# Two experts' main rows computed during the last routing, in a hybrid decoder step with a mixture of experts

## What is computed

```python
def moe(h, w_router, b_router, w_gate, w_up, w_down):
    aff = sigmoid(h @ w_router)                       # 16 experts in 4 groups
    biased = aff + b_router
    gscore = top_k(biased.reshape(n, 4, 4), 2)[0].sum(-1)
    in_group = ... == argmax(gscore, -1)[:, None]     # one group a token
    _, idx = top_k(where(in_group, biased, NEG_INF), 2)
    w_sel = take_along_axis(aff, idx, -1); w_sel /= w_sel.sum(-1)
    ...
    hid = silu(a) * b * gates                         # a = h @ w_gate[e], b = h @ w_up[e]
    return einsum('nef,efd->nd', hid, w_down)

h = layer_norm(ALPHA * x + mix @ w_out)               # mix: attention, state space, pooling
y = layer_norm(ALPHA * h + moe(h))
```

## Time and profile before

| | |
|---|---|
| median of 3 runs | 997.49 us (997.23 to 998.46) |
| the profiled execution | 994.33 us, span 992.6 us |
| TensorE (PE) | busy 912.7 us, 92% of the span |
| VectorE (DVE) | busy 423.7 us, 43% |
| ScalarE (ACT) | busy 311.8 us, 31% |
| GpSimd (POOL) | busy 212.7 us, 21% |
| mean granted PE clock | 0.978 of full |
| DMA | 173.23 MB, 175 GB/s in the mean |

### The profile page before, as it was taken

How to read it: one execution, slowest core, us unless ns; L and a number is a source line. 1 busy time by engine, 2 the same in 40 slices (tenths; PEclk the granted TensorE clock), 3 DMA queues, 4 the chain that set the end, 5 groups by cost and what they waited for, 6 DMA issues and landing times.

```text
span 992.6 us, 13623 instructions
## 1 busy us (share of the span) xinstructions
PE 912.7 (92%) x5025; PEld 579.4 (58%) x5025; DVE 423.7 (43%) x1244; ACT 311.8 (31%) x631; POOL 212.7 (21%) x289
## 2 busy tenths in 40 slices
PE   4999999999999999999899999994899999999785
PEld 4655645555566666666554444532788887878321
DVE  5689799612344343345424326648100001010156
ACT  6751505612233233225414233431212121211222
POOL 3089000011101346651021100432000000000155
PEclk9999999999999999999999999996999999999888
DMA  9540000465982025216441131457976888966293
GB/s 232 156 182 1 2 0 2 143 188 168 413 352 88 22 77 181 107 64 226 159 171 45 43 87 45 169 207 279 318 244 242 319 301 288 380 220 254 95 373 138
DMA packets 63677, 173.23 MB, mean 175 GB/s; under 512 B 17416, under 2 KB 26687, under 8 KB 58103
## 3 DMA queue, kind: packets, MB, share of 16 engines
q1 hardware_dynamic: 55047, 141.37, 41.0%
q0 software_dynamic: 8368, 30.41, 8.4%
q10 hardware_dynamic: 192, 0.52, 0.2%
HBM read 113.24 MB, written 59.11 MB: 174 GB/s over the span
## 4 chain that ended last, share of the span: by engine, by line
PE 43%; DVE 3%; ACT 2%; DMA 1%; issue 1%; ACTq 0%; POOL 0%; DVEq 0%
PE banks L2350 14%; PE banks L2185 11%; PE banks L2363 6%; PE banks L2465 2%; PE banks L2344 2%; PE banks L2376 1%; PE banks L2482 1%; PE banks L2296 1%; PE banks L2197 1%; PE banks L2269 1%; PE banks L2250 1%; PE banks L2217 1%; DVE xT L2744 0%; DMA x_slots<-xT,slot_i 0%; DVE arena L2814 0%
## 5 line engine op out<-in xcount | busy, mean ns | idle before, releaser
L1514 PE MATMUL banks<-xT,arena 128*128 128x384 f32 (+2 forms) x384 | 122.9, 475 | 5.7 <-DVE mx L1709 3.8
L2185 PE MATMUL banks<-arena,mixT 128*128 128x512 f32 x256 | 116.8, 602 | 0.0
L1514 PEld LDWEIGHTS banks<-xT,arena 128*128 128x128 f32 x384 | 71.4, 190 | 53.6 <-DVE mx L1709 10.5
L2185 PEld LDWEIGHTS banks<-arena,mixT 128*128 128x128 f32 x256 | 47.0, 193 | 49.5 <-issue 49.5
L2350 PEld LDWEIGHTS banks<-mixT,arena 128*128 128x128 f32 x512 | 70.4, 190 | 6.8 <-issue 6.8
L2350 PEld LDWEIGHTS banks<-mixT,v_tok 128*128 128x128 f32 x512 | 70.3, 190 | 4.3 <-issue 4.3
L2350 PE MATMUL banks<-mixT,arena 128*128 128x160 f32 x512 | 71.7, 300 | 0.8 <-ACT mixT L2564 0.8
L2350 PE MATMUL banks<-mixT,v_tok 128*128 128x160 f32 x512 | 70.9, 299 | 0.8 <-ACT mixT L2564 0.8
L2721 POOL DMA_INDIRECT arena<-y_park,slot_s x17 | 16.2, 951 | 250.6 <-DMA y_park<-arena 245.7
L1619 ACT ACTIVATE arena<-arena,mx 128x144 f32<-128x144 f32 (+7 forms) x64 | 50.2, 785 | 62.5 <-DVE mx L1709 62.1
L535 PE MATMUL banks<-mixT,xT 128*128 128x512 f32 x144 | 62.7, 594 | 0.0
(11 more groups left out here) (413 smaller groups left out, 1367.5 us busy)
## 6 DMA issues: line engine op xcount, KB each, us to landing
arena<-in_w_down SPq DMA_DIRECT2D x16, 1024.0 KB, 8.4
x_slots<-xT SPq DMA_DIRECT2D x4, 2048.0 KB, 15.4
y_park<-xT SPq DMA_DIRECT2D x4, 2048.0 KB, 32.5
v_tok<-in_w_gate SPq DMA_DIRECT2D x8, 1024.0 KB, 7.0
v_tok<-in_w_up SPq DMA_DIRECT2D x8, 1024.0 KB, 7.0
arena<-in_w_gate SPq DMA_DIRECT2D x8, 1024.0 KB, 6.4
arena<-in_w_up SPq DMA_DIRECT2D x8, 1024.0 KB, 8.6
arena<-x_slots SPq DMA_DIRECT2D x16, 512.0 KB, 5.3
```

What stands on the lines that cost most here:

```text
L1514: last = T.matmul(b[:, 0:cn], w[:, k, :], xT[:, k, c0:c0 + cn], start=(k == 0), stop=(k == KD - 1))
L2185: last = T.matmul(bank[half], mixT[:, k, META + t * P:META + (t + 1) * P], w_oh[half][:, k, :], start=(k == 0), stop=(k == KD - 1))
```

## The change

- Batches become (0, 4), (4, 6), (6, 7), (7, 9). `choose(2)` and `slots(2)`, now for tile 6 alone, come into DVE's turn of tile 7; PE's `ranks(1)` and `ranks(2)` come into tile 7, and tile 6's two scatters follow directly on those of tiles 4 and 5 on POOL. The last batch has tiles 7 and 8.
- For experts 0 and 1 (`FIRST = 2`) the 128 main places are for tiles 0 to 6; before batch 3 their counts are raised to 128, so tiles 7 and 8 (and what is beyond 128) go to the 32 last places.
- The samples' projection writes banks 6 and 7, not 0 and 1, and no longer waits for tile 7's residual.
- SP loads the main rows of experts 0 and 1 as soon as tiles 0 to 6 are scattered, behind three of the weight loads; PE turns the rows of expert 0 ahead of tile 8, runs its gate matmuls between the steps of tile 8's routing, then its up matmuls, `ranks(3)`, expert 1 and both down passes, all on 128 rows. The eight idle matmuls are gone.
- The 32 last rows of experts 0 and 1 are then computed together, with the weights moving and the rows standing (`first_rests`): four groups (gate and up of both) side by side. The product is transposed back (`turn_first_rests`) and put beside the other hidden rows.
- Buffers for this: expert 2's gate and up weights have their own places; the gate and up weights of experts 3 and 4 wait for `first_rests`; main rows of experts 0 to 3 have buffers of their own. All four loads of rest rows of the first group are issued on SP (two were on ACT). The second norm's gain and shift are loaded later.
- At the end ACT makes `scaled_i` and the 18 `dg` before expert 15's silu; PE runs `residual` of tiles 1, 3 and 0 before the overflow block, as their banks come free, and of tile 2 after it. The square root table is loaded ahead. Tile 8's second norm is done in two DVE passes, without ACT's.
- At the start `centre(1)` comes before `dt_rows`, and `copy_high(0)` before `stats(2)`.

```diff
-NOV = 2 * TOKM // (CAP + 1)
+FIRST = 2
+NOV = FIRST + (2 * TOKM - FIRST * (REM + 1)) // (CAP + 1)
...
                 stats(1)
+                centre(1)
                 dt_rows()
-                centre(1)
+                copy_high(0)
                 stats(2)
-                copy_high(0)
...
-            BATCH = ((0, 4), (4, 6), (6, 8), (8, 9))
+            BATCH = ((0, 4), (4, 6), (6, 7), (7, 9))
+            EARLY = BATCH[2][1]
...
                 def load_gate(e):
-                    if e >= 2:
+                    if e == 2:
+                        sp.wait_ge(s_mm, NT)
+                    elif 3 <= e <= 4:
+                        sp.wait_ge(s_fr, 1)
+                    elif e >= 5:
                         sp.wait_ge(s_gt, e - 1)
...
                 def load_rows(e):
-                    if e >= 2:
+                    if e < FIRST:
+                        sp.wait_ge(s_sct, 16 * 2 * EARLY)
+                        sp.wait_ge(s_mm, NQ)
+                    elif e < 4:
+                        sp.wait_ge(s_sct, 16 * 2 * NT)
...
                 load_gate(0)
                 load_up(0)
                 load_gate(1)
+                load_rows(0)
+                load_rows(1)
                 load_up(1)
                 load_down(0)
                 load_down(1)
+                load_gate(2)
+                load_up(2)
+                load_down(2)
+                load_rest(0)
+                load_rows(2)
+                load_down(3)
+                load_rows(3)
+                store(0)
+                store(1)
+                load_gate(3)
+                load_up(3)
+                load_rest(1)
+                load_gate(4)
+                load_up(4)
...
+                def first_rests():
+                    pe.wait_ge(s_hid, FIRST)
+                    for k in range(KD):
+                        for which in range(2):
+                            for e in range(FIRST):
+                                g = 2 * which + e
+                                last = T.matmul(bank[2][REM * g:REM * (g + 1), 0:DE], xall[:, e, k, MAIN:CAP],
+                                                (gate_w, up_w)[which](e)[:, k * DE:(k + 1) * DE],
+                                                start=(k == 0), stop=(k == KD - 1), tile_position=(0, REM * g))
+                    last.then_inc(s_fr, 1)
...
+                t = NT - 2
+                turn(t - 1)
+                project(t, 0)
+                route_parts(t - 1)
+                turn_probabilities(3)
+                ranks(1)
+                project(t, 1, slice(0, 2))
+                route(t - 1)
+                project(t, 1, slice(2, 4))
+                weigh(3)
+                project(t, 2)
+                turn_outputs(3)
+                ranks(2)
+                project(t, 3)
+                t = NT - 1
+                project(t, 0)
+                project(t, 1)
+                turn(t - 1)
+                project(t, 2)
+                route_parts(t - 1)
+                project(t, 3)
+                route(t - 1)
+                pe.wait_ge(s_xe[0], 16)
+                turn_rows(0, xe[0])
+                turn(t)
+                pe.wait_ge(s_gw[0], 16)
+                pe.wait_ge(s_xc, 2)
+                pe.wait_ge(s_res, NT)
+                gate_or_up(0, 0, js=(0,))
+                route_parts(t)
+                gate_or_up(0, 0, js=(1,), ks=range(0, 4))
+                route(t)
+                gate_or_up(0, 0, js=(1,), ks=range(4, KD)).then_inc(s_gt, 1)
+                pe.wait_ge(s_xe[1], 16)
+                turn_rows(1, xe[1])
+                pe.wait_ge(s_uw[0], 16)
+                gate_or_up(0, 1).then_inc(s_up, 1)
                 ranks(3)
-                for n in range(8):
-                    T.matmul(bank[n % 2], ident[:, :], mixT[:, 0, META:META + 512], start=True, stop=True)
...
+                gate_or_up(1, 0).then_inc(s_gt, 1)
+                pe.wait_ge(s_uw[1], 16)
+                gate_or_up(1, 1).then_inc(s_up, 1)
+                down(0)
+                down(1)
                 pe.wait_ge(s_xr, 64)
...
+                turn_rows(rest_no(0), xr)
+                pe.wait_ge(s_xe[2], 16)
+                turn_rows(turn_no(2), xe[2])
+                pe.wait_ge(s_xc, 2 * rest_no(0) + 2)
+                first_rests()
...
                 pe.wait_ge(s_al, 1)
-                for t in range(4):
-                    residual(t)
+                residual(1)
+                pe.wait_ge(s_yA, out_no(E - 1))
+                pe.wait_ge(s_yD, out_no(E - 1))
+                residual(3)
...
+                residual(0)
...
+                overflow(pe, released, body, done)
+
+                residual(2)
...
+                S.activation(ln[2][:, 18:19], ident[:, 0:1], ACT.Sqrt).then_inc(s_tl, 1)
+                act.wait_ge(s_mm, NT)
+                copy_rows(0)
+                x_turned(NT - 1)
+                deviation(NT - 1)
+                S.activation(ln[2][:, 19:20], ident[:, 0:1], ACT.Exp).then_inc(s_tl, 1)
+                take_parts(NT - 1)
+                take_logits(NT - 1)
+                copy_rows(1)
+                silu(0)
+                silu(1)
+                low(0, ys[0])
+                low(1, ys[1])
...
+                    if t0 == EARLY:
+
+                        chain(V.scalar_tensor_tensor(prior[:, t0, 0:FIRST], cap16[:, 0:FIRST], float(MAIN),
+                                                     prior[:, t0, 0:FIRST], ALU.add, ALU.max))
...
-                    if t == 8:
-                        choose(2, residual_samples)
+                    if t == 7:
+                        choose(2)
                     if dec and t % 2:
                         outputs(d)
+                    if t == 7:
+                        slots(2)
...
+                hidden(0)
                 weights(2)
                 weights(3)
                 overflow_table()
+                hidden(1)
...
+                high(0, ys[0])
+                high(1, ys[1])
```

More of the change, by code:

```diff
@@ L1891, in hybrid_step @@
             hid = [mall[:, at + 2 * CAP * n:at + 2 * CAP * (n + 1)].rearrange("p (j n) -> p j n", j=2) for n in range(6)]
+            at += 12 * CAP
+            sil = [mall[:, at + 2 * CAP * n:at + 2 * CAP * (n + 1)] for n in range(2)]
+            at += 4 * CAP
+            hr = mall[HP:P, at:at + DE]
+            assert 7 * TP <= at - 4 * CAP and at - 7 * TP <= META + SEQ and at + DE <= KD * TP
+            xe = [mixT[:, 3, 0:D], mixT[:, 4, 0:D], gb[:, 0, :], gb[:, 1, :]]
+            assert 3 * TP >= 2 * KD * CAP
             gate_src = A["w_gate"][0].rearrange("e (p k) f -> e p (k f)", p=P)
@@ L2183, in project @@
                     else:
-                        for k in range(4 * (quarter % 2), 4 * (quarter % 2) + 4):
+                        for k in range(4 * (quarter % 2), 4 * (quarter % 2) + 4)[part_]:
                             last = T.matmul(bank[half], mixT[:, k, META + t * P:META + (t + 1) * P],
@@ L2379, in down_rest @@
                     last.then_inc(s_dn, 1)
-                for t in range(NT):
-                    d, dec = t // 2, t < BS
-                    if dec and t % 2 == 0:
+                for t in range(NT - 2):
+                    d = t // 2
+                    if t % 2 == 0:
                         turn_keys(d, 0)
@@ L2444, in _, with residual @@
                 down_rest(E // 4 - 1)
+                def residual(t):
+                    if t - 4 in SHIFT_DVE:
+                        pe.wait_ge(s_yv, shifted_no(t - 4))
+                    elif t >= 4:
+                        pe.wait_ge(s_gn2, t - 3)
+                    for half in range(2):
+                        cols = slice(512 * half, 512 * half + 512)
+                        T.matmul(duo[t % 4][:, cols], scaled_i, h_all[:, t, cols],
+                                 start=True, stop=False)
+                pe.wait_ge(s_al, 1)
+                residual(1)
+                pe.wait_ge(s_yA, out_no(E - 1))
+                pe.wait_ge(s_yD, out_no(E - 1))
+                residual(3)
+                pe.wait_ge(s_yA, out_no(E - 1) + 1)
+                pe.wait_ge(s_yD, out_no(E - 1) + 1)
+                residual(0)
                 pe.wait_ge(s_yA, out_no(E - 1) + 2)
@@ L2973, in _ @@
                 measure(NT - 1)
-                slots(2)
                 scale_shift(NT - 1)
```

309 lines of the change are left out of this document (184 added, 125 removed).

## The result

The changed kernel takes **1303.05 us** (median of 4 runs, 1299.4 to 1308.31) beside 997.36 (996.5 to 998.46) for the kernel before: 1.308 times as long, interval 1.304 to 1.312. The forecast was 969.4 us, 963.5 to 976.5. The profiled execution took 1308.31 us, with a span of 1306.6.

A forecast was written before the change was run, and what follows sets the result against it. PE (TensorE) was taken as busy nearly everywhere, its largest hole where the last tokens are routed. Gains 1.4 + 20.7 + 6.0 = 28.1 us off 997.5 gave 969.4 us, range 963.5 to 976.5.

The forecast's parts named there:

- the parts don't fit: Experts 0 and 1 drawing over 128 early or 32 late rows would run the overflow pass; called excluded, no chance given.
- slower than before: Last tokens' routing: expert 0's rows landing past 700.6 would lose the gain; at 703 the time is 1000; chance 0.02.
- Start: First tiles: tile 1 given first lets PE turn it 1.5 to 2.0 us earlier; gain kept 1.4 (0 to 2.0).
- The cover named there: Early in the kernel DVE meets a load at 37.75 that the change doesn't move, so not all of 1.5 to 2.0 is kept.
- Middle: Last tokens' routing up to expert 3's gate: work of experts 0 and 1 fills PE's hole; gain 20.7 us.
- rows come late: Tile 6's scatter needs the whole 9.0 us, expert 0's rows at 675.1; 2.6 us less gain, 972.0; chance 0.25.
- the forecast's own sign of being wrong: In routing, PE waiting over 3 us for expert 0's rows, tile 6's ranks or expert 3's weights.
- Clock: Near 670, where PE has only transposes, its clock falls; this decides 2.3 us of the routing gain.
- New stalls: Late weights of experts 3 and 4 cost 2.1; with a low tail and no start gain, 974.8; chance 0.11.
- Tail: After the experts: residuals in PE's standing time, tile 0 3.5 us sooner, shorter last tile; gain 6.0 (4.1 to 7.6).
- the old hole: Kernel before, samples' output projection to expert 0's first gate matmul: 33.5 us, with PE busy for 16.9.
- alone: Scatters with no weight loads beside them, taken to land in 3.8 us, against 9.0 beside six weight loads.

The follow-up runs named there:

- the version with real rows: Changed kernel with the last batch's ranks and counts taking 64 rows for tile 8, so its padding rows aren't counted; 970.33 us, 971.88 when run again.
- the run with earlier rows: Against the version with real rows: expert 1's gate weights loaded behind experts 0 and 1's first rows, expert 2's rows issued from ACT's queue; 973.03 us.

## Why the prediction was wrong, and where it was right

**The step that failed** is the last rival, *the parts don't fit*: "excluded". In its place the overflow pass ran for two experts and cost 332.7 us (1303.05 against 970.33 with real rows counted). The working there was a count of the reference's own choices for experts 0 and 1. It asked whether real tokens fit their places and took for granted that the kernel counts only these. It didn't follow the new batch into `ranks`, where the number of rows goes by a batch's first tile, and it looked at the two experts that the change handles, not at 13 and 14, which stand at 159 and 157 of 160 and needed two and four more. So a chance of nothing stood on a branch whose price, 166 us an expert, the trace of before couldn't show. The 0.02 for slower than before stood for late rows.

**The rest of the sum** can be checked on the version with real rows. Stretches of the kernel before that answer to it, from the last quarter of tile 7's projection: to expert 3's gate, to the last rest rows, to tile 0's weights, to the end.

```profile
656.00:740.48 84.48, 65.69 (x366) 47.01 (x365) 34.18 (x136) 19.09 (x38) 10.92 (x10) 0.90 0.83 298
740.48:929.32 188.84, 187.31 (x1162) 150.84 (x1160) 18.11 (x30) 33.17 (x78) 0.00 (x0) 1.00 0.75 270
929.32:949.10 19.78, 13.34 (x50) 4.88 (x49) 1.38 (x2) 5.78 (x21) 8.00 (x9) 0.83 0.59 193
949.10:992.60 43.50, 29.08 (x89) 8.80 (x88) 31.04 (x66) 13.69 (x19) 22.24 (x15) 0.84 0.63 246
```

The same stretches with real rows:

```profile
656.90:723.14 66.24, 57.22 (x416) 41.92 (x416) 30.79 (x115) 20.06 (x40) 8.00 (x7) 0.97 0.87 311
723.14:912.11 188.97, 187.25 (x1161) 150.84 (x1161) 17.42 (x29) 36.90 (x96) 0.00 (x0) 1.00 0.78 287
912.11:928.77 16.66, 10.94 (x49) 3.83 (x49) 1.38 (x2) 2.66 (x4) 5.73 (x6) 0.95 0.52 163
928.77:970.10 41.33, 28.88 (x88) 8.83 (x88) 30.66 (x65) 11.24 (x17) 24.46 (x17) 0.83 0.73 285
```

- *Start, 1.4 (0 to 2.0)*: nothing. PE's first long projection starts at 15.46 in place of 17.14, as forecast, but DVE then meets tile 6's input, the load of the earlier trace rows, at 39.29 and not 37.75 (37.9 to 42.3 in the nine other profiles of the new order), and at 50 us PE is level with before (50.11 and 49.91). The last quarter of tile 7's projection begins 0.9 later (0.2 in the second profile of this version). The cover named there took all of it.
- *Middle, 20.7 (17 to 23)*: 84.48 - 66.24 = 18.2; 18.9 in the second profile of this version (65.57). The steps, on the timeline of the version with real rows:

```profile
660.88 0.96 POOL L2857 DMA_INDIRECT x_slots<-xT,slot_i  x1 [0.30 <-issue]
671.14 0.80 SPq L2130 DMA_DIRECT2D mixT<-x_slots  x2
674.81 1.97 PE L2421 MATMUL banks<-ident,mixT 128*128 128x128 f32 x8 [4.99 <-DMA mixT<-x_slots]
692.10 0.98 POOL L2857 DMA_INDIRECT x_slots<-xT,slot_i  x1 [19.26 <-DVE slot_i L3074]
699.82 1.92 SPq L2140 DMA_DIRECT2D arena<-x_slots  x4
704.77 1.16 PE L2421 MATMUL banks<-ident,arena 128*128 128x128 f32 x8
707.39 1.16 PE L2421 MATMUL banks<-ident,gb 128*128 128x128 f32 x8 [1.46 <-DMA gb<-x_slots]
712.07 4.61 PE L2430 MATMUL banks<-mixT,arena 128*128 128x160 f32 x32
723.14 8.93 PE L2430 MATMUL banks<-mixT,arena 128*128 128x160 f32 x64 [0.77 <-issue]
```

  The scatter of tile 6 went out when forecast (660.8) but took 10.3 us until SP could load, not 6.4: beyond the long end of 9.0, the way of the rival *rows come late*. With three weight loads beside it, it took 9.9 to 10.3 in seven profiles, with two 8.3 to 8.9 in three (8.5, from 662.13 to 670.63, in the run with earlier rows). Rows landed in 3.7 in place of 5.3, so PE turned them at 674.8 (672.5 forecast, 0.9 of it the start's). The last scatters landed at 699.8 (697.6), the rest rows were turned at 704.8 (702.6), and the wait for expert 2's rows, the fifth load in a row from SP, cost 1.5 us that the step had left out. Rest matmuls 3.6, as forecast; from expert 2's gate to expert 3's 11.1 (10.7).
  PE waited 5.0 us for expert 0's rows, so the forecast's own sign of being wrong, more than 3 us there, came true. The sign was set too tight: the sum itself had PE free at 669 and the rows at 672.5.
- *Clock*: it fell where forecast, 0.78 from 674.81 to 682.32, and was worth 1.3 in the mean, 2.6 in the pair of profiles above (2.3).
- *New stalls*: expert 3's weights were in time; the stage behind it kept its length, 188.97 and 188.84.
- *Tail, 6.0 (4.1 to 7.6)*: 3.1 to tile 0's weights (3.5), which do wait for the gather, and 2.2 behind them (2.5), 5.3.

Two readings were loose, without weight in the sum: PE waits for DVE a second time in the old hole, 5.6 us ahead of tile 8's ranks, and two of the six scatters taken for "alone" in the earlier trace rows went out behind two loads of 512 KB.

Together 18.2 + 5.3 - 0.9 - 0.1 = 22.5, the difference of the two spans (25.1 with the second profile); by the medians of its two series 27.3 and 24.8, where 28.1 were forecast. Without the pass the time, 970.33 and 971.88, lies inside the range. The rival in first place behind the forecast, late rows with 972.0, describes it best.

## What to carry to other kernels

Where a change regroups tiles, look for each size that is taken from a group's first member; a partial tile that joins a full one brings its padding along, and results can stay the same while a count that steers a branch doesn't. Price each data-dependent branch, and note how far the data stand from it (here 159 and 157 of 160), before calling it excluded. In a chain of loads, bringing one forward paid here only until the next load in the queue bound, and the load on a second queue took from the one needed first.

## What was not expected of the hardware

A wait of 2.0 us on PE (expert 4's rows) was followed by a granted clock of 0.50 in 731 to 733 and cost the next eight records 5.29 - 3.60 = 1.7 us, as four of them at half clock would; 3.0 us (rest rows beside a second queue) were followed by about 6.7 us at half clock, worked out from granted clocks of 0.84 in 700 to 712 and 0.89 in 712 to 725. But the length of the wait alone doesn't decide it: behind the 2.6 us that the kernel before waits for its first rows the clock stayed at 1.00 (700.01 to 712.50). And in the overflow pass the same three waits a tile, of 1.25, 1.09 and 0.83 us, went with the lower clock in two tiles of one run and in ten and twelve of others.

The times of one version spread by 5 to 9 us in series of five runs and more (968.0 to 975.1, 994.3 to 1002.8), as much as the smaller terms of the sum; those could be read only from stretches that start at a common point.
